# Feed-forward input tiles: both parts of the input as one moving operand of 512 columns, two PSUM banks a tile

## The reference

```python
def conv_ffn(x, w_in, conv_w, conv_b, w_out):
    gate, up = jnp.split(x @ w_in, 2, axis=-1)
    gp = jnp.pad(gate, ((0, 0), (CONV_W - 1, 0), (0, 0)))
    gc = conv_b
    for j in range(CONV_W):
        gc = gc + gp[:, j:j + T, :] * conv_w[j]
    h = jax.nn.gelu(gc) * up
    return h @ w_out
...
ffn = (jax.nn.silu(gate) * up) @ w_down[i]
```

## Time and profile before

| | us |
|---|---|
| median of 3 runs | 1112.05 (1111.98 to 1114.02) |
| profiled execution, its own time | 1112.02 |
| its span in the trace | 1110.2 |
| TensorE matmuls busy | 1090.4 (8121 matmuls) |
| weight loads busy | 991.0 |
| VectorE busy | 767.8 |
| ScalarE busy | 548.4 |
| GpSimd busy | 202.4 |

### The profile page before, as it was taken

How to read it: one execution, slowest core, us unless ns; L and a number is a source line. 1 busy time by engine, 2 the same in 40 slices (tenths; PEclk the granted TensorE clock), 3 DMA queues, 4 the chain that set the end, 5 groups by cost and what they waited for, 6 DMA issues and landing times.

```text
span 1110.2 us, 20201 instructions
## 1 busy us (share of the span) xinstructions
PE 1090.4 (98%) x8121; PEld 991.0 (89%) x8121; DVE 767.8 (69%) x1062; ACT 548.4 (49%) x776; POOL 202.4 (18%) x230
## 2 busy tenths in 40 slices
PE   7999999999999999999999999999999999999997
PEld 6997898999998789989999988998777789999986
DVE  7997888777775658857777646688868775444443
ACT  6765355543343567845344344645665445333332
POOL 0125452122210011002112200470100001221100
PEclk9999999999999999999999999999999999999999
DMA  8553162646666466345666574556452554666552
GB/s 233 176 174 114 44 225 78 172 128 179 186 189 249 162 156 152 113 108 158 190 184 178 178 283 147 175 190 211 141 143 85 191 165 130 180 188 189 190 190 76
DMA packets 219750, 183.16 MB, mean 165 GB/s; under 512 B 43265, under 2 KB 197614, under 8 KB 219678
## 3 DMA queue, kind: packets, MB, share of 16 engines
q1 hardware_dynamic: 215566, 171.36, 51.6%
q0 software_dynamic: 3392, 8.66, 2.4%
q10 hardware_dynamic: 720, 2.13, 0.5%
HBM read 179.44 MB, written 2.69 MB: 164 GB/s over the span
## 4 chain that ended last, share of the span: by engine, by line
PE 83%; DVE 9%; DMA 2%; ACT 2%; issue 2%; POOL 1%; SPq 0%; DVEq 0%; POOLq 0%; ACTq 0%
PE bank L280 23%; PE bank L282 23%; PE bank L281 23%; PE bank L288 2%; DVE ring L401 2%; PE bank L1181 1%; PE bank L1322 1%; PE bank L359 1%; ACT arena L395 1%; PE bank L373 1%; DMA ring<-in_w_out 1%; DVE arena L1678 1%; DVE stat L1676 1%; PE bank L1305 1%; DMA ring<-in_a_w_rkv 1%
## 5 line engine op out<-in xcount | busy, mean ns | idle before, releaser
L280 PE MATMUL bank<-arena,arena 128*128 128x256 f32 (+2 forms) x1868 | 593.4, 318 | 1.6 <-DVE ring L401 1.3
L395 ACT ACTIVATE arena<-ring 128x2048 fp32r<-128x2048 f32 (+1 forms) x143 | 269.2, 1884 | 292.1 <-DMA ring<-in_ffn_w_in 109.4
L401 DVE TENSOR_TENSOR ring<-ring,arena 128x2048 fp32r<-128x2048 f32 (+1 forms) x136 | 305.5, 2249 | 150.8 <-ACT arena L395 150.0
L280 PEld LDWEIGHTS bank<-arena,arena 128*128 128x128 f32 x1868 | 356.0, 191 | 25.3 <-DVE ring L401 2.2
L281 PE MATMUL bank<-arena,arena 128*128 128x256 f32 (+1 forms) x1308 | 373.3, 285 | 0.0
L282 PE MATMUL bank<-arena,ring 128*128 128x256 f32 x1220 | 345.2, 283 | 0.0
L281 PEld LDWEIGHTS bank<-arena,arena 128*128 128x128 f32 x1308 | 250.8, 192 | 1.1
L282 PE MATMUL bank<-arena,arena 128*128 128x512 f32 (+3 forms) x644 | 239.3, 372 | 0.0
L282 PEld LDWEIGHTS bank<-arena,ring 128*128 128x128 f32 x1220 | 234.1, 192 | 0.0
L281 PE MATMUL bank<-ring,arena 128*128 128x512 f32 (+2 forms) x560 | 216.2, 386 | 0.0
L282 PEld LDWEIGHTS bank<-arena,arena 128*128 128x128 f32 x644 | 121.2, 188 | 20.9
(11 more groups left out here) (350 smaller groups left out, 1288.1 us busy)
## 6 DMA issues: line engine op xcount, KB each, us to landing
ring<-in_ffn_w_in SPq DMA_DIRECT2D x80, 512.0 KB, 5.0
ring<-in_ffn_w_out SPq DMA_DIRECT2D x44, 512.0 KB, 4.4
ring<-in_w_gate_up SPq DMA_DIRECT2D x40, 512.0 KB, 5.0
ring<-in_w_in SPq DMA_DIRECT2D x18, 1024.0 KB, 5.2
ring<-in_a_w_rkv SPq DMA_DIRECT2D x12, 1024.0 KB, 5.4
ring<-in_w_down SPq DMA_DIRECT2D x22, 512.0 KB, 3.7
ring<-in_a_w_o SPq DMA_DIRECT2D x4, 1024.0 KB, 8.2
arena<-in_ffn_w_in SPq DMA_DIRECT2D x8, 512.0 KB, 4.7
```

The source lines that it names most:

```text
L280: nc.tensor.matmul(dst, stationary[0], moving[0], start=start, stop=False)
L395: nc.scalar.activation(buf(hi_of(n), 0, w, arena12), ring[:, r, 0:w], ACT.Copy).then_inc(hi_ready, 1)
L401: on.tensor_tensor(ring12[:, r, 0:w], ring[:, r, 0:w], buf(hi_of(n), 0, w, arena12).bitcast(F32), ALU.subtract).then_inc(split_ready, 1)
```

## The change

The hi and lo buffers of the activations become one array (`arena12`), so that `beside` can name both as one operand of 2 x 256 columns. The step for one chunk is two matmuls in place of three, and gate and up have a bank each: after the tile the left half of a bank holds hi x hi + lo x hi, and the right half hi x lo. ScalarE copies the right halves out, VectorE adds the left halves to them (`whole_sum`), and everything behind reads the sum from SBUF. The last tap goes to ScalarE, as a copy with a scale, and the bias into the GELU. VectorE's product of a tile moves behind the additions of the next tile. In the loop TensorE alternates between banks 2, 3 and 0, 1, and waits for the additions (`conv_step`) of the tile two before. The early tiles and the output halves keep their matmuls.

```diff
-        arena12 = [sb(f"arena12_{i}", [P, n, SLOT], F32R) for i, n in ARENA]
+        arena12 = [sb("arena12", [P, sum(n for _, n in ARENA), SLOT], F32R)]
...
+        def product_twice(dst, stationary, hi, both_parts, start, stop):
+
+            nc.tensor.matmul(dst[:, :], stationary[0], both_parts, start=start, stop=False)
+            return nc.tensor.matmul(dst[:, 0:T], stationary[1], hi, start=False, stop=stop)
...
+        def beside(i, j):
+
+            i, j = sorted((i, j))
+            return arena12[0][:, i:j + 1:j - i, :].rearrange("p s (c t) -> p s c t", t=T)
...
+        whole_sum = [[buf(FFN_P, (RING + 2 * g + s) * T, (RING + 2 * g + s + 1) * T) for s in range(2)] for g in range(2)]
...
+        FIRST_SEATS, SEATS = (1, 3, 0, 2), (1, 0, 1, 0)
...
                 pe.wait_ge(split_ready, SPLIT_NO[first + j] + 1 + it * RING)
-                if seat_taken(it, j):
-                    pe.wait_ge(ffn_prod, f * FC + it * RING + (j + EARLY - RING + 1))
+                if not isinstance(it, int):
+                    pe.wait_ge(conv_step, tile_step(f, it, j - 2, 2))
+                elif j == 2:
+                    pe.wait_ge(ffn_prod, f * FC + EARLY)
+                pair = 2 * (FIRST_SEATS if isinstance(it, int) else SEATS)[j]
...
-                        mm = product(bank[seat(j)][:, g * T:(g + 1) * T], both(w, slice(None), k, g), both(h2, slice(None), k),
-                                     k == 0, k == DC - 1)
+                        mm = product_twice(bank[pair + g], both(w, slice(None), k, g), h2[0][:, k], h_parts[:, :, k],
+                                           k == 0, k == DC - 1)
...
         def ffn_act(act, f):
...
             def tile(it, j):
-                split_act(act, first + AHEAD + j, it)
+                pair = 2 * (FIRST_SEATS if isinstance(it, int) else SEATS)[j]
+                act.wait_ge(slot_done, first + it * RING + (j + 1))
+                nc.scalar.activation(whole_sum[0][j % 2], bank[pair][:, T:2 * T], ACT.Copy).then_inc(act_done, 1)
+                if f == 2 and (j >= 2 or not isinstance(it, int)):
+                    act.wait_ge(ffn_prod, f * FC + it * RING + (EARLY + j - 1))
+                nc.scalar.activation(whole_sum[1][j % 2], bank[pair + 1][:, T:2 * T], ACT.Copy).then_inc(act_done, 1)
+                act.wait_ge(conv_step, tile_step(f, it, j, 1))
                 if f < 2:
...
+                    nc.scalar.activation(conv_acc[seat(j)], whole_sum[0][j % 2], ACT.Copy,
+                                         scale=conv_at(f, it, j, (f"ffn_conv_w{f}", 2 * FC))).then_inc(act_done, 1)
+                    split_act(act, first + AHEAD + j, it)
+                    act.wait_ge(conv_step, tile_step(f, it, j, 4))
+                    nc.scalar.activation(gate_act[seat(j)], conv_acc[seat(j)], ACT.Gelu_apprx_tanh,
+                                         bias=conv_at(f, it, j, ("ffn_conv_b", f * FC))).then_inc(act_done, 1)
                 else:
...
+                    nc.scalar.activation(gate_act[seat(j)], whole_sum[0][j % 2], ACT.Silu).then_inc(act_done, 1)
+                    split_act(act, first + AHEAD + j, it)
...
         def ffn_dve(dve, f):
...
+            def multiplied(it, j):
+                dve.wait_ge(act_done, tile_act(f, it, j, 4 if f < 2 else 3))
+                dve.wait_ge(conv_step, tile_step(f, it, j, 2))
+                if seat_taken(it, j):
+                    dve.wait_ge(ffn_done, f * FC + it * RING + (j + EARLY - RING + 1))
+                nc.vector.tensor_tensor(gated[seat(j)], gate_act[seat(j)], whole_sum[1][j % 2], ALU.mult).then_inc(ffn_prod, 1)
...
+                gate, conv = whole_sum[0][j % 2], conv_acc[seat(j)]
+                for g in range(2):
+                    dve.wait_ge(act_done, tile_act(f, it, j, g + 1))
+                    nc.vector.tensor_tensor(whole_sum[g][j % 2], bank[pair + g][:, 0:T], whole_sum[g][j % 2],
+                                            ALU.add).then_inc(conv_step, 1)
+                if j > 0:
+                    multiplied(it, j - 1)
+                elif not isinstance(it, int):
+                    multiplied(it - 1, RING - 1)
                 if f < 2:
-                    dve.wait_ge(slot_done, first + it * RING + (j + 1))
-                    nc.vector.tensor_scalar(conv, gate, at(it, j, tap[2]), at(it, j, ("ffn_conv_b", f * FC)),
-                                            ALU.mult, ALU.add).then_inc(conv_step, 1)
+                    dve.wait_ge(act_done, tile_act(f, it, j, 3))
                     for i in (1, 0):
...
                 split_dve(dve, first + AHEAD + j, it)
-                dve.wait_ge(act_done, f * FC + it * RING + (j + EARLY + 1))
-                if seat_taken(it, j):
-                    dve.wait_ge(ffn_done, f * FC + it * RING + (j + EARLY - RING + 1))
-                nc.vector.tensor_tensor(gated[seat(j)], gate_act[seat(j)], up, ALU.mult).then_inc(ffn_prod, 1)
...
             rounds(dve, tile)
+            multiplied(LOOPS - 1, RING - 1)
```

40 lines of the change are left out of this document (24 added, 16 removed).

## The result

| | before | after | forecast |
|---|---|---|---|
| median of the runs | 1112.84 us (4 runs, 1111.98 to 1114.02) | 1102.74 us (4 runs, 1100.60 to 1104.69) | 1099.3 us |
| ratio | | 0.9913, 95% interval 0.9901 to 0.9925 | 1099.3 / 1112.05 = 0.9885 |
| profiled execution | 1112.02 us | 1104.69 us | 1099.2 us |

The change is faster by 10.1 us by the medians and by 7.33 us between the two profiled executions; 12.8 us were forecast. The direction and the kind of gain are as forecast. The time is 3.4 us above the forecast, outside its own range and just inside the wide one (1097.5 to 1103.0). The rest of this document is about those few microseconds.

A forecast was written before the change was run, and what follows sets the result against it. TensorE's matmuls were taken as the bound in the input halves: 0.213 us saved a tile, 4.27 per 20 tiles, 12.8 for three feed-forwards, from 1112.05 to 1099.3 us. Own range 1098.3 to 1101.5; 8 in 10, 1097.5 to 1103.

The forecast's parts named there:

- What bounds the kernel: Feed-forward input halves: TensorE busy 116.00 of 116 us, so a matmul removed or shortened there is time gained.
- The fixed 0.0133 us of a matmul: Input halves: each matmul costs about 0.0133 us beyond its columns; one fewer per step saves 12.8 us in all.
- rival 3: TensorE matmuls: only a small fixed cost each, 2.5 ns by the skill's rule, giving 1109.6 us; chance 2%.
- an alternating stream has each border as often as the other, so I keep 0.3467: Input-half steps: lone width borders, 0.007 under and 0.013 over the sum, leave a step at 0.3467 us.
- up to 1112: Input halves: the two-piece operand costs a step up to 0.360 us again, time up to 1112 us; chance 5%.
- The moving operand in two pieces at no cost: Input-half 512-column matmuls: an operand in two pieces slots apart adds nothing; at most another 0.0133 us each.
- The round of ScalarE and VectorE: Input-half tiles: first addition to first addition takes 5.3 us against 5.547 a tile, so it fits by 0.25.
- VectorE's own path: Input-half tiles: VectorE's taps end at 3.0 us after a tile's last matmul, before ScalarE's weight copy at 3.4.
- rival 2: Input halves: the ScalarE and VectorE round becomes the bound at 6.43 us, total 1137 us; chance 4%.
- Output slot 4: First feed-forward's output half: slot lands 15.8 us after the input half, ready about 20.1, needed at 21.8; hidden.
- rival 4: Gain partly given back by a late output slot or a lag at the stage's end, 1102 to 1109 us; chance 3%.
- 123.5 us: Length of an input half if VectorE paid for all of GpSimd's work, stated as 8.3 us more than now.

The follow-up runs named there:

- e4: Changed kernel with the first side weights of the first two feed-forwards' output halves loaded after output slot 4 instead of before: 1101.34 us, ratio 0.9894.
- e3: Changed kernel with the 512-column matmuls reading two neighbouring chunks of the rounded part, one contiguous piece (output wrong): 1102.49 us, ratio 0.9907.
- e5: Changed kernel with matmul order 512, 256, 256, 512, so equal widths come in pairs: 1102.04 us, ratio 0.9918.
- e2: Changed kernel with eight 512-column matmuls, then eight of 256, for gate and for up, instead of alternating: 1102.51 us, ratio 0.9911.
- e1: The changed kernel run again, nothing edited: 1104.31 us, ratio 0.9932.
- e7: Changed kernel without GpSimd's difference; the output half multiplies the rounded part in place of the low part: 1101.42 us (one run).
- e8: Changed kernel with ScalarE's scaled copy repeated once more per tile, unused, in the first two feed-forwards: 1103.58 us (one run).
- e10: The changed kernel run a third time, nothing edited: 1103.68 us, ratio 0.9924.
- e11: e4 run again (changed kernel, side weights loaded after output slot 4): 1104.76 us, ratio 0.9929.
- e9: Changed kernel with ScalarE's scaled copy repeated three more times per tile, unused, in the first two feed-forwards: 1136.08 us (one run).

## Why the prediction was right, and where it was wrong

1. **What bounds the kernel** was right: TensorE busy for 95.00 of 95.00 us in every window, before and after; 960 fewer matmuls are time gained.
2. **The fixed 0.0133 us of a matmul** was right for the fast rhythm; in the slow one a removed matmul is worth 0.360 - 0.3533 = 0.0067. The fast halves take 111.25 us against 111.2 forecast, and the lowest runs, 1099.54 (e4) and 1099.71 (e3), and 1100.29 in paired order (e5), come near the 1099.3. The Trainium skill's 2.5 ns for a warm matmul (TensorE: Matmul & The Clock Gate, Back-to-back issue gap) would have given 2.4 us for three feed-forwards; the gain is 10.1, so the trace speaks against it for this kind of matmul, and rival 3 falls.
3. **The step that failed** is this sentence: "an alternating stream has each border as often as the other, so I keep 0.3467". The two borders were read where they stand alone, to 0.01 us, over one matmul each, and put at nothing in sum. In e2, where they can be followed, a change to 512 columns and back costs 20 ns over seven matmuls. The alternating stream has two prices, 0.3467 and 0.3533 us a step, and a half takes one or the other for all its 320 steps. In the eight profiled executions of alternating kernels whose TensorE waits for no input tile (after, e1, e3, e4, e7, e8, e10, e11), 10 of 24 input halves were slow. As an estimate from these counts, that is 3 x 10/24 x 2.1 = 2.6 us in the mean, most of the 3.4 us by which the median missed. The same eight executions bear it out: less 2.1 us for each slow half, they took 1099.3 to 1101.5. The runs without a trace say less. All 13 runs of the changed kernel spread from 1100.60 to 1106.45 with a mean of 1103.7, and the kernel before, whose three halves in its trace are all alike, itself spreads from 1110.82 to 1114.85. So the rhythms are not the whole scatter, and one or two microseconds of the miss stay without an account. In the terms of the sum: 12.8 us should have stood as 6.4 to 12.8 with its middle near 10. The range was too narrow for the same reason, since it let no case in between the forecast and "up to 1112".
4. **The moving operand in two pieces at no cost** was right for the alternating order (e3). In groups, too: the 512s away from a border take 226 to 227 ns, the price of one piece (e2).
5. **The round of ScalarE and VectorE** was right in sum (5.19 us for 5.3) and in its path, which goes through ScalarE's scaled copy and weight copy. VectorE's own path was reckoned to be 0.4 us ahead at the difference (3.0 against 3.4) and is level with it: the taps take 1.64 us and not 1.1, now that they read SBUF twice beside GpSimd. In the earlier trace rows GpSimd was the one that paid; here VectorE pays too, 0.483 to 0.621 and 0.481 to 0.673. The Trainium skill (SBUF — State Buffer, Who interferes with whom) has them share one port pair as an exclusive lock; the runs agree in kind (e7), in both directions. GpSimd's difference that began at 341.89 behind VectorE's of 341.61 took 2.61 us for 0.73 (e8), and in the first trace VectorE's weight difference that began at 344.00 behind GpSimd's of 343.83 took 2.71 for 2.29. Had GpSimd's work all been added, as rival 2 put it, the round would have been 6.43; the cost was 0.33 us of VectorE's time, hidden beside ScalarE's weight copy.
6. **Output slot 4** was sized right, and its cover was as thin as stated. SP's wait for GpSimd ends at 344.60, 7.66 us after the half, against 6.19 before (345.02): 1.5 later, for 1.7 forecast. Before, ScalarE came to the slot at 353.08, which is 14.25 us after the half and not the 14.1 of the prediction. It came 16.4 us after it in the first trace and 15.7 in e1_same: 2.1 and 1.5 later. In the first feed-forward slot 4 stays hidden in both. The slots behind it are loaded after it, and at the ninth TensorE waits in all three traces: 0.65 us before, 0.55 in e1_same, and 1.34 in the first trace, which is its loss of 0.70 us in output half 1. In the second feed-forward of the first trace ScalarE came to slot 4 17.8 us after the half, and there TensorE, whose matmuls otherwise start 0.227 apart, lost 0.27 us (646.04 to 646.54). In e1_same, 16.7 us after, it lost nothing. So the cover was nearly used up, and how much is lost changes from execution to execution: rival 4, in part. TensorE at the ninth slot in the first trace:

```profile
382.02 0.50 PE L282 MATMUL bank<-arena 128*128 128x512 f32 x1 [1.34 <-DVE ring L413]
```

7. **Rival 2** did not come by itself but was priced at about half of what it costs: e9 shows the lag paid in the input half and again in the output half, there with some 2 us of a halved clock in it. Two sums of the prediction are also off, without effect on the forecast: 123.5 us is 8.0 more than 115.48, not 8.3, so that three halves make 24 and not 25; and 0.83 + 0.41 + 1.1 + 2.29 is 4.63, not 4.65.

Open: what picks the rhythm. It is not the half's place (e1, e7, e8, e10), nor the shape of the moving operand (e3), nor a wait, the clock or the DMA share, and it is settled before the half's first matmul (e1). In the slow rhythm the three steps differ although their instructions do not, so it looks like a stream that locks to something with a period of its own; that is argued from the numbers, not shown. Also open are why a change of width costs what it does, and the run of e5_snake at 1107.04.

## What to carry to other kernels

Price a stream of mixed widths from a steady stream of that mix, never from lone borders at the resolution of the trace: count the matmuls in a window in which the engine never idles, and do it in several executions, since one trace shows one draw. Where an order is free, prefer one that gave the same time in every stage (equal widths next to each other here) to one with two rhythms, even if its best case is 0.5 us worse. And a lag that a stage's buffers hide is not free: ask who starts late when the stage ends, and look at the granted clock behind the wait.

## What the hardware showed that was not expected

- The same instructions, with no wait and at granted clock 1.00, ran in two steady rhythms, 0.3467 and 0.3533 us for a 512 and a 256, each held for 113 us and chosen anew in each execution (10 of 24 halves slow). The starts just ahead of a half tell which it will be: 228 or 229 ns over two matmuls before a fast one, 230 to 234 before a slow one, 24 of 24. Orders with the two widths in pairs (nine halves of 111.77 to 111.79 us) and in groups of eight (three of 112.03 or 112.04) had one time each, however they began.
- In the alternating stream a 512 takes 231 to 240 ns until the next matmul starts and a 256 only 113 to 120, where steady streams have 227 and 120: some of the wide one's time is given back by the narrow one. In groups of eight, a change to 512 columns is felt over five matmuls (233, 236, 228, 233, 231 ns, then 227).
- VectorE, too, is slowed when both of its inputs are in SBUF and GpSimd works: in the mean from 0.483 to 0.621 us for the tap that mostly meets a cast and from 0.481 to 0.673 for the one that mostly meets a difference, and 0.486 when that difference is gone. With one input in PSUM, in the kernel before, a tap beside GpSimd's difference stayed at 0.48.
- After TensorE had stood still for 5.26 and for 4.6 us (e9), its matmuls of 512 columns were 427 ns apart for about 5 us, at granted clock 0.50.
